# Where the last embedding product, the first gate product and the per-tile roots stand in the closing stage of a one-core decoder layer

## The chip, the cores and the metric

The kernel runs on one core of a Trainium2 chip. A core has TensorE (PE, matrix products), VectorE (DVE), ScalarE (ACT), GpSimd (POOL) and SyncE (SP, which issues most transfers); each runs its own instruction list in order, and they wait for one another through semaphores. The metric is the device time of the whole program in microseconds (us), as the median of several executions.

## The reference, cut to what matters

The program computes one decoder layer on x (512 tokens, 1024 channels): a mixing part (convolution and attention, then an output projection), a mixture of 32 experts with two per token, a gated embedding, and a last normalisation. The change lies in the last two:

```python
x = x + hier_moe(rms_norm(x, g_ffn[i]), ...)
gate = jax.nn.sigmoid(rms_norm(x, g_ple[i]) @ w_ple_gate[i] + b_ple_gate[i])
x = x + (p[i] @ w_ple_proj[i]) * gate
return rms_norm(x, g_final)
```

`p[i]` is 512 x 256, `w_ple_proj` 256 x 1024, `w_ple_gate` 1024 x 1024. `rms_norm` squares and sums a token's 1024 channels, takes the root of the mean plus a small number, and divides.

## The kernel before, in words

Tokens are cut into four tiles of 128 (t = 0 to 3), channels of an output into two halves of 512. Every engine's list is written out by hand; nothing is reordered by a scheduler, so the order in the code is the order on the engine. PSUM, where PE writes its products, is eight banks of 128 x 512; a table fixes which product uses which bank, and each bank has a semaphore for full and one for free.

The expert stage is a loop of passes. The last pass ends with the down products of PE (L1793). ACT and DVE copy their two banks to SBUF (L964, L1428), POOL scatters them to a buffer y_d in HBM, and SP reads y_d back as sorted rows (L701), four tiles of two parts. The closing stage is then:

- PE waits for both copies (`ya_ready`, `yd_ready`), and computes eight embedding products `ple(q)`, q = 0 to 7 (L1816, of two channel blocks each; q // 2 is the tile). ACT copies each out (L932).
- DVE adds the two expert parts to a tile of x (L1453, two instructions a tile). PE transposes the tile's rows (`turn_x2(t)`, L1848, eight transposes into two banks). ACT copies the transposed rows out rounded (x2_hi, L983), and DVE writes what the rounding left (x2_lo, L1460). ACT then squares and sums the tile and takes its root (`mean_root`, L800 and L802).
- PE computes eight gate products `product(q)` (L1837): q // 4 is the channel half and q % 4 the tile. Each is three groups of eight matmuls: high rows by high weights, low rows by high weights, high rows by low weights. The weights of a half are split into high and low by `split_gate` of ACT (L972) and of DVE (L1443). For the first half this lies before the embedding copies; for the second it comes on ACT behind the fourth tile's root, and on DVE behind its x2_lo. DVE handles no gate product before that second split is done.
- For each gate product, DVE multiplies by the tile's reciprocal root and adds the bias (L1488, which waits for the bank and frees it); ACT takes the sigmoid (L1003); DVE multiplies by the embedding (L1491) and adds to x (L1494); ACT squares and sums the 512 channels (`square_out`, L992).
- Once both halves of a tile are squared, ACT takes its last root (`final_root_of`, L999), and DVE its reciprocal (L1021) and two scalings of 512 columns (`final_out`, L1475); SP sends each of them out (L709).

Before, ACT takes the root of tile t one product late: behind the sigmoid of product 4 + t + 1, ahead of that product's square. DVE calls `final_out(t)` at the end of that same step, and so handles the next bank without waiting for a root in between. The sigmoid and the root lie in different activation tables, and an ACT_TABLE_LOAD stands where the function changes.

Of the kernel before, what the change touches and what calls it, by code (L numbers as in the profile page):

```python
# [55 lines left out]
FIXED = 3  # L56
SLOTS = 3
STRAIGHT = NE // 2 - 2
DOWN_PARTS = (2, 2, 4)
PAIRS = NE // 2  # L60
SORTED = PAIRS - FIXED
# [153 lines left out]
def build(nc, x, w_in, w_out, w_r, w_gate, w_up, w_down, w_pg, w_pp, pT, b_pg, g_final, prm, cst, out):  # L215
    ctx = ExitStack()
    with ctx:
        def sb(name, shape, dt=F32):
            return ctx.enter_context(nc.sbuf_tensor(name, shape, dt))
# [5 lines left out]
        def sem(name):  # L225
            return ctx.enter_context(nc.semaphore(name))
# [10 lines left out]
        xs = sb("xs", [P, TT, D])  # L237
# [27 lines left out]
        by8 = sb("by8", [P, 9, 2 * TT])  # L265
        gw = sb("gw", [P, 2, TT])
        sqh = sb("sqh", [P, 2, TT])
        key_col = sb("key_col", [P, 2])
        order = sb("order", [1, MOST, 2], I32)

# [56 lines left out]
        junk = ar(12288, D)  # L327
# [167 lines left out]
        xhi_ready = sem("xhi_ready")  # L495
        gated = sem("gated")
        squared = sem("squared")
        half_ready = sem("half_ready")
        final_root = sem("final_root")
        x3_ready = sem("x3_ready")  # L500
        o_ready = sem("o_ready")
# [290 lines left out]
        def _(act):  # L792
# [5 lines left out]
            def mean_root(which, t, unused):  # L798

                act.activation(unused, xs[:, t, :], ACT.Square, accum_out=sq[:, which, t:t + 1]).then_inc(root_ready, 1)  # L800
                act.wait_ge(root_ready, 2 * (which * TT + t) + 1)
                act.activation(ss[:, which, t:t + 1], sq[:, which, t:t + 1], ACT.Sqrt, scale=1.0 / D, bias=eps[:]).then_inc(root_ready, 1)  # L802
# [170 lines left out]
                                   scale=pr[:, Q_PLE + k:Q_PLE + k + 1]).then_inc(whi_ready, 1)  # L973

            split_gate(0)
            for q in range(2 * TT):
                ple_out(q)

            act.wait_ge(gathered[0], 16 * half + 16)
            for t in range(TT):  # L980
                for kh in range(2):
                    banks.wait_full(act, ("x2", t, kh))
                    act.activation(x2_hi[:, 4 * kh:4 * kh + 4, t * P:(t + 1) * P],  # L983
                                   bk(("x2", t, kh))[:].rearrange("p (k n) -> p k n", k=4), ACT.Copy).then_inc(xhi_ready, 1)
                mean_root(2, t, junk)
            split_gate(1)
            def square_out(q):

                half, t = q // TT, q % TT
                act.wait_ge(x3_ready, 2 * (q + 1))  # L990
                wait(act, squared, q)
                act.activation(junk[:, 0:512], xs[:, t, half * 512:(half + 1) * 512], ACT.Square, scale=1.0 / 32,  # L992
                               accum_out=sqh[:, half, t:t + 1]).then_inc(squared, 1)

            def final_root_of(t):

                act.wait_ge(half_ready, 1)
                act.wait_ge(squared, TT + t + 1)
                act.activation(ss[:, 3, t:t + 1], sqh[:, 1, t:t + 1], ACT.Sqrt, bias=sq[:, 3, t:t + 1]).then_inc(final_root, 1)  # L999

            for q in range(2 * TT):
                banks.wait_emptied(act, ("pgate", q))
                act.activation(sgate[:, q % 4, :], sgate[:, q % 4, :], ACT.Sigmoid).then_inc(gated, 1)  # L1003
                if q > TT:
                    final_root_of(q - TT - 1)
                square_out(q)
            final_root_of(TT - 1)


        @block.vector  # L1010
        def _(dve):
# [456 lines left out]
            def final_out(t):  # L1468

                if t == 0:  # L1470
                    dve.wait_ge(last_loaded, 16)
                dve.wait_ge(final_root, t + 1)
                recip(rs[:, 3, t:t + 1], ss[:, 3, t:t + 1])
                for cols in (slice(0, 512), slice(512, D)):
                    dve.scalar_tensor_tensor(out=xn_rows[:, t, cols], in0=xs[:, t, cols], scalar=rs[:, 3, t:t + 1],  # L1475
                                             in1=gfin[:, cols], op0=ALU.mult, op1=ALU.mult).then_inc(o_ready, 1)

            x3 = 0
            for q in range(2 * TT):
                half, t = q // TT, q % TT  # L1480
                name = ("pgate", q)
                cols = slice(half * 512, (half + 1) * 512)
                banks.wait_full(dve, name)
                if q == 0:
                    dve.wait_ge(bias_loaded, 16)
                if q >= 4:
                    dve.wait_ge(x3_ready, 2 * (q - 3))
                emptied(dve.scalar_tensor_tensor(out=sgate[:, q % 4, :], in0=bk(name)[:], scalar=rs[:, 2, t:t + 1],  # L1488
                                                 in1=brow[:, cols], op0=ALU.mult, op1=ALU.add), name)
                dve.wait_ge(gated, q + 1)  # L1490
                dve.tensor_tensor(sgate[:, q % 4, :], sgate[:, q % 4, :], plep[:, t, cols], ALU.mult).then_inc(x3_ready, 1)  # L1491
                x3 += 1
                dve.wait_ge(x3_ready, x3)
                dve.tensor_tensor(xs[:, t, cols], xs[:, t, cols], sgate[:, q % 4, :], ALU.add).then_inc(x3_ready, 1)  # L1494
                x3 += 1
                if q == TT:
                    dve.wait_ge(squared, TT)
                    dve.tensor_scalar(sq[:, 3, :], sqh[:, 0, :], EPS, None, ALU.add).then_inc(half_ready, 1)
                if q > TT:
                    final_out(t - 1)  # L1500
            final_out(TT - 1)


# [1 line left out]
        def _(pe):  # L1505
# [318 lines left out]
            def product(q):  # L1824

                half, t = q // TT, q % TT
                name = ("pgate", q)
                if t == 0:
                    pe.wait_ge(whi_ready, (half + 1) * DK)
                banks.wait_free(pe, name)  # L1830
                parts = ((wpg_hi[half], 0), (wpg_hi[half], 1), (wpg_lo[half], 0))
                for j, (w, rest) in enumerate(parts):
                    if t == 0 and j == 2:
                        pe.wait_ge(wlo_ready, (half + 1) * DK)
                    for k in range(DK):
                        lhs = x2_lo[t][:, k, :] if rest else x2_hi[:, k, t * P:(t + 1) * P]
                        ins = pe.matmul(bk(name)[:], lhs, w[:, k, :], start=(j == 0 and k == 0),  # L1837
                                        stop=(j == 2 and k == DK - 1))
                filled(ins, name)
# [49 lines left out]
```

## Time and profile before

| | us |
|---|---|
| median of 3 runs | 584.1 |
| lowest and highest | 583.13, 586.76 |
| the profiled execution | 583.52 |
| its span in the profile | 581.7 |
| PE busy | 505.3 (87%) |
| DVE busy | 294.8 (51%) |
| ACT busy | 184.9 (32%) |

The span runs from the first to the last recorded instruction; the execution's own time is 1.82 us longer. Busy shares are averages over stages with different limits. The closing stage, from the end of the last down product to the end of the span, takes the last 72 us. All times in the rows further down are counted from the start of the span.

### The profile page before, as it was taken

The numbers are of one execution on the slowest core, as the hardware profiler recorded it, in microseconds if no ns is written. First come the engines' busy times: TensorE is split into PE (matmuls) and PEld (weight loads), VectorE is DVE, ScalarE is ACT, GpSimd is POOL, SyncE is SP. The second block draws the span as 40 slices with busy tenths as digits, with TensorE's granted clock in tenths as the row PEclk, the third lists the DMA queues.
The fourth block names the chain that finished last, engine by engine and source line by source line (L and its number), as shares of the span: only waits on it lengthen the run. The fifth ranks groups of instructions, "written<-read, shape, count | busy, mean of one in ns | idle before, by whom it ended". The sixth has DMA issues, their size and how long they took to land.

```text
span 581.7 us, 8775 instructions
## 1 busy us (share of the span) xinstructions
PE 505.3 (87%) x3193; PEld 300.1 (52%) x3193; DVE 294.8 (51%) x558; ACT 184.9 (32%) x355; POOL 78.2 (13%) x91
## 2 busy tenths in 40 slices
PE   4999999997889979958999996887877888899994
PEld 4788888774556658854433332232222222237883
DVE  4329899999996963476221211111011111167676
ACT  6821411337775352332010100000000000066755
POOL 0740000000032040010211122011111001010000
PEclk9999999999889979988999999988888999899998
DMA  9931300445506065396999999999999899958003
GB/s 311 372 134 33 118 15 16 148 158 168 216 2 272 1 246 225 132 409 232 341 404 418 418 421 421 415 418 419 396 412 413 367 394 415 355 212 344 1 1 144
DMA packets 38071, 150.31 MB, mean 258 GB/s; under 512 B 5905, under 2 KB 10513, under 8 KB 26257
## 3 DMA queue, kind: packets, MB, share of 16 engines
q1 hardware_dynamic: 32416, 139.14, 61.3%
q0 software_dynamic: 5328, 10.50, 4.9%
q8 instruction: 25, 0.41, 0.3%
q10 hardware_dynamic: 288, 0.15, 0.1%
q14 instruction: 14, 0.11, 0.0%
HBM read 142.95 MB, written 14.68 MB: 271 GB/s over the span
## 4 chain that ended last, share of the span: by engine, by line
PE 53%; SPq 16%; DMA 12%; DVE 8%; ACT 5%; issue 4%; POOL 1%; DVEq 0%; POOLq 0%; ACTq 0%
PE bank L1528 15%; PE bank L1773 10%; DMA wring<-w_up_in 8%; PE bank L1837 8%; SPq L583 7%; PE bank L1630 5%; PE bank L1793 4%; PE bank L1554 4%; SPq L511 3%; SPq L603 2%; DMA wring<-w_in_in 2%; SPq L598 1%; PE bank L1671 1%; DMA wring<-y_d 1%; PE bank L1761 1%
## 5 line engine op out<-in xcount | busy, mean ns | idle before, releaser
L1773 PE MATMUL bank<-wring,arena 128*32 128x512 f32 x656 | 87.4, 658 | 19.9 <-DMA wring<-w_up_in 17.7
L1071 DVE SCALAR_TENSOR_TENSOR mix<-arena,pr,mix 128x512 f32<-128x512 f32 x120 | 85.6, 781 | 0.0
L1423 DVE TENSOR_TENSOR arena<-arena,bank 128x256 f32<-128x256 f32 x16 | 6.7, 421 | 138.7 <-ACT arena L958 138.7
L1773 PEld LDWEIGHTS bank<-wring,arena 128*32 128x32 f32 x656 | 25.8, 119 | 75.2 <-issue 68.7
L958 ACT ACTIVATE arena<-bank 128x256 f32<-128x256 f32 x16 | 6.2, 384 | 140.1 <-PE bank L1773 140.1
L1773 PE MATMUL bank<-mix,arena 128*32 128x512 f32 x240 | 38.6, 639 | 7.6 <-DMA arena<-w_up_in 7.6
L1793 PE MATMUL bank<-wring,arena 128*32 128x512 f32 x352 | 40.0, 595 | 5.3 <-ACT arena L961 5.3
L1773 PE MATMUL bank<-arena 128*32 128x512 f32 x80 | 38.6, 638 | 0.0
L1428 DVE COPY arena<-bank 128x512 f32<-128x512 f32 x16 | 11.1, 692 | 53.5 <-PE bank L1793 53.5
L1528 PE MATMUL bank<-hT_hi,win_hi 128*128 128x512 f32 x128 | 33.5, 398 | 1.2 <-DVE hT_lo L1049 0.6
L1528 PE MATMUL bank<-hT_lo,win_hi 128*128 128x512 f32 x128 | 31.7, 389 | 0.0
L1528 PE MATMUL bank<-hT_hi,win_lo 128*128 128x512 f32 x128 | 31.6, 389 | 0.0
L964 ACT ACTIVATE arena<-bank 128x512 f32<-128x512 f32 x16 | 9.6, 597 | 60.8 <-PE bank L1793 60.8
L1773 PEld LDWEIGHTS bank<-mix,arena 128*32 128x32 f32 x240 | 10.8, 116 | 34.6 <-issue 31.4
L1528 PEld LDWEIGHTS bank<-hT_hi,win_hi 128*128 128x128 f32 x128 | 23.6, 188 | 9.5 <-ACT hT_hi L820 1.9
L1528 PEld LDWEIGHTS bank<-hT_lo,win_hi 128*128 128x128 f32 x128 | 24.0, 188 | 5.0
L1528 PEld LDWEIGHTS bank<-hT_hi,win_lo 128*128 128x128 f32 x128 | 24.0, 188 | 5.0
L765 POOL COPY ycur<-tlist 128x1 int32 x16 | 2.9, 182 | 169.0 <-DVE arena L1428 169.0
L1793 PEld LDWEIGHTS bank<-wring,arena 128*32 128x32 f32 x352 | 10.3, 109 | 27.6 <-issue 20.5
L725 POOL TENSOR_TENSOR mixa_lo<-mix,mixa_hi 128x512 fp32r<-128x512 f32 x4 | 5.6, 1405 | 134.9 <-ACT mix L881 134.9
L1761 PEld LDWEIGHTS bank<-c,arena 128*128 128x128 f32 x136 | 15.3, 146 | 13.0 <-issue 12.6
L815 ACT ACTIVATE win_hi<-wring 128x1024 fp32r<-128x1024 f32 x20 | 20.0, 1072 | 5.5 <-DMA wring<-w_in_in 5.5
(260 smaller groups left out, 916.0 us busy)
## 6 DMA issues: line engine op xcount, KB each, us to landing
wring<-w_down_in SPq DMA_DIRECT2D x22, 1024.0 KB, 20.3
wring<-w_gate_in SPq DMA_DIRECT2D x21, 1024.0 KB, 15.5
wring<-w_up_in SPq DMA_DIRECT2D x21, 1024.0 KB, 19.1
wring<-w_in_in SPq DMA_DIRECT2D x3, 2048.0 KB, 14.5
arena<-w_down_in SPq DMA_DIRECT2D x5, 1024.0 KB, 13.8
mix<-w_up_in SPq DMA_DIRECT2D x5, 1024.0 KB, 13.1
arena<-w_up_in SPq DMA_DIRECT2D x5, 1024.0 KB, 20.1
mix<-w_gate_in SPq DMA_DIRECT2D x5, 1024.0 KB, 16.6
```

Of the source, the lines that this page charges most:

```text
L511: return eng.value_load(ap, min_val=least, max_val=most)
L583: sp.dma_start(up_w(w, a)[:, i], (w_gate, w_up)[i][bass.ds(expert(n, a), 1)].rearrange("e (p k) n -> p (e k) n", k=DK)).then_inc(up_loaded ...
L603: sp.dma_start(dn_w(w, a), src).then_inc(dn_loaded[w], 16)
L815: act.activation(win_hi[i][:, :, cols], win[i][:, :, cols], ACT.Copy).then_inc(win_hi_ready[i], 1)
L1071: ins = dve.scalar_tensor_tensor(out=mixc[:, mm, :], in0=u[:, mm, j:j + S], scalar=w, in1=mixc[:, mm, :], op0=ALU.mult, op1=ALU.add)
L1528: ins = pe.matmul(bk(name)[:], w[:, k, m * P:(m + 1) * P], h[:, k, :], start=(j == 0 and k == 0), stop=(j == 2 and k == DK - 1))
L1554: ins = pe.matmul(bk(("v", t))[:], h[:, k, t * P:(t + 1) * P], w[:, k, :], start=(j == 0 and k == 0), stop=(j == 2 and k == DK - 1))
L1630: ins = pe.matmul(bk(name)[:], src[:, m, t * P:(t + 1) * P], weight[:, m, half * 512:(half + 1) * 512], start=(j == 0), stop=(j == 3 * CM ...
L1761: ins = pe.transpose(pb[k // 4][:, k % 4 * P:(k % 4 + 1) * P], xg[:, s, k * P:(k + 1) * P], ident)
L1773: ins = pe.matmul(pb[2 + s][lo:hi, :], xgT[:, s, k, lo:hi], weights[:, :, k, :], start=(k == 0), stop=(k == DK - 1))
L1793: ins = pe.matmul(pb[6 + half][lo:hi, :], hidT[:, s, k, lo:hi], dn_cols(w, a, k, half), start=(k == 0), stop=(k == FK - 1))
L1837: ins = pe.matmul(bk(name)[:], lhs, w[:, k, :], start=(j == 0 and k == 0), stop=(j == 2 and k == DK - 1))
```

## The change

On PE, the waits for the two copies move from ahead of the first embedding product to ahead of the third (`ya_ready`) and the fourth (`yd_ready`). These are the products that write the banks concerned. The eighth embedding product moves behind the first tile's transposes. Each tile's transposes move behind the first group of the preceding tile's gate product, and the waits for x2_hi and x2_lo become separate.

```order
L1816 MATMUL bank<-wring 128x512 x16
L1848 MATMUL bank<-c,xs 128x128 x16
L1837 MATMUL bank<-wpg_hi_70,x_hi 128x512 x8
L1837 MATMUL bank<-wpg_hi_70,x_lo_75 128x512 x8
L1837 MATMUL bank<-wpg_lo_72,x_hi 128x512 x8
L1848 MATMUL bank<-c,xs 128x128 x8
L1837 MATMUL bank<-wpg_hi_70,x_hi 128x512 x8
```

Above is PE before, from the end of the expert loop; below is PE after the change, from the same place (L1857 are the embedding products, L1901 the transposes, L1889 the gate products).

```order
L1857 MATMUL bank<-wring 128x512 x4
L1864 REGISTER_ALU
L1857 MATMUL bank<-wring 128x512 x10
L1901 MATMUL bank<-c,xs 128x128 x8
L1857 MATMUL bank<-wring 128x512 x2
L1889 MATMUL bank<-wpg_hi_70,x_hi 128x512 x8
L1901 MATMUL bank<-c,xs 128x128 x8
L1889 MATMUL bank<-wpg_hi_70,x_lo_75 128x512 x8
L1889 MATMUL bank<-wpg_lo_72,x_hi 128x512 x8
```

The sixteen transposes in a row became eight and eight, with one embedding product and one group of a gate product in between; the number of matmuls is the same.

On ACT the root of a tile moves into the step of its own square, behind a small Sqrt that reads nothing new and calls for the table. The next two fences are ACT from the sigmoid of product 5 to the root of tile 1, before and after (L1003 and L1007 are the sigmoids, L992 and L996 the squares, L999 and L1003 of the second fence the roots, L1009 the small Sqrt).

```order
L1003 ACTIVATE wring<-wring 128x512
L999 ACT_TABLE_LOAD
L999 ACTIVATE ss<-sqh,sq 128x1
L992 ACTIVATE arena,sqh<-xs 128x512
L1003 ACT_TABLE_LOAD
L1003 ACTIVATE wring<-wring 128x512
L999 ACT_TABLE_LOAD
L999 ACTIVATE ss<-sqh,sq 128x1
```

After the change:

```order
L1007 ACTIVATE wring<-wring 128x512
L1009 ACT_TABLE_LOAD
L1009 ACTIVATE unused<-eps 128x1
L996 ACTIVATE arena,sqh<-xs 128x512
L1003 ACTIVATE ss<-sqh,sq 128x1
L1007 ACT_TABLE_LOAD
L1007 ACTIVATE wring<-wring 128x512
```

The root moved from ahead of a square to behind it.

On DVE the reciprocal and the two scalings of a tile move one product earlier: from behind the steps of the product that follows the tile's own second half, to ahead of them. Product 7 is handled in two parts of 256 columns. First DVE before, from the last addition of product 3 to the bias step of product 5, then the same stretch after the change (L1488 and L1510 are the bias steps, L1494 and L1516 the additions to x, L1498 and L1520 the constants from the first halves).

```order
L1494 TENSOR_TENSOR xs<-xs,wring 128x512
L1488 SCALAR_TENSOR_TENSOR wring<-bank,rs,wring 128x512
L1491 TENSOR_TENSOR wring<-wring,mix 128x512
L1494 TENSOR_TENSOR xs<-xs,wring 128x512
L1498 TENSOR_SCALAR sq<-sqh 128x4
L1488 SCALAR_TENSOR_TENSOR wring<-bank,rs,wring 128x512
```

After the change:

```order
L1516 TENSOR_TENSOR xs<-xs,wring 128x512
L1520 TENSOR_SCALAR sq<-sqh 128x4
L1510 SCALAR_TENSOR_TENSOR wring<-bank,rs,wring 128x512
L1513 TENSOR_TENSOR wring<-wring,mix 128x512
L1516 TENSOR_TENSOR xs<-xs,wring 128x512
L1041 RECIPROCAL rs<-ss 128x1
L1495 SCALAR_TENSOR_TENSOR arena<-xs,rs,wring 128x512 x2
L1510 SCALAR_TENSOR_TENSOR wring<-bank,rs,wring 128x512
```

The constants moved ahead of product 4, where they wait for the square of product 3; and the reciprocal and the scalings of tile 0, which waited for a root behind product 5, now stand ahead of the bias step of product 5.

The diff, cut to its core:

```diff
@@ ACT
-            for q in range(2 * TT):
+            for q in range(2 * TT - 1):
                 ple_out(q)
...
+                if t == 0:
+                    ple_out(2 * TT - 1)
                 mean_root(2, t, junk)
...
-                act.wait_ge(half_ready, 1)
-                act.wait_ge(squared, TT + t + 1)
+                act.wait_ge(half_ready, 1 if t < TT - 1 else 2)
+                act.wait_ge(squared, TT + t + 1 if t < TT - 1 else LAST + 2)
...
-            for q in range(2 * TT):
+            for q in range(LAST):
                 banks.wait_emptied(act, ("pgate", q))
                 act.activation(sgate[:, q % 4, :], sgate[:, q % 4, :], ACT.Sigmoid).then_inc(gated, 1)
-                if q > TT:
-                    final_root_of(q - TT - 1)
+                if q >= TT:
+                    act.activation(unused[:], eps[:], ACT.Sqrt)
                 square_out(q)
+                if q >= TT:
+                    final_root_of(q - TT)
+
+            for part in range(2):
+                cols = slice(part * 256, (part + 1) * 256)
+                if part == 0:
+                    act.wait_ge(part_ready, 1)
+                else:
+                    banks.wait_emptied(act, ("pgate", LAST))
+                act.activation(sgate[:, LAST % 4, cols], sgate[:, LAST % 4, cols], ACT.Sigmoid).then_inc(gated, 1)
+            act.activation(unused[:], eps[:], ACT.Sqrt)
+            for part in range(2):
+                act.wait_ge(x3_ready, 2 * (LAST + part + 1))
+                act.wait_ge(squared, LAST + part)
+                act.activation(junk[:, 0:256], xs[:, TT - 1, 512 + part * 256:768 + part * 256], ACT.Square, ...)
             final_root_of(TT - 1)
@@ DVE
-            for q in range(2 * TT):
+            for q in range(LAST):
                 half, t = q // TT, q % TT
                 name = ("pgate", q)
+                if q > TT:
+                    final_out(t - 1)
...
-                if q == TT:
+                if q == TT - 1:
                     dve.wait_ge(squared, TT)
                     dve.tensor_scalar(sq[:, 3, :], sqh[:, 0, :], EPS, None, ALU.add).then_inc(half_ready, 1)
-                if q > TT:
-                    final_out(t - 1)
+
+            final_out(TT - 2)
+            name, b = ("pgate", LAST), LAST % 4
+            banks.wait_full(dve, name)
...
+            for part in range(2):
+                cols = slice(part * 256, (part + 1) * 256)
+                ins = dve.scalar_tensor_tensor(out=sgate[:, b, cols], in0=bk(name)[:, cols], ...)
...
+            for part in range(2):
...
+                dve.wait_ge(gated, LAST + part + 1)
+                dve.tensor_tensor(sgate[:, b, cols], sgate[:, b, cols], plep[:, TT - 1, there], ALU.mult).then_inc(x3_ready, 1)
+                dve.wait_ge(x3_ready, x3 + 1)
+                dve.tensor_tensor(xs[:, TT - 1, there], xs[:, TT - 1, there], sgate[:, b, cols], ALU.add).then_inc(x3_ready, 1)
+                x3 += 2
+            dve.wait_ge(half_ready, 1)
+            dve.wait_ge(squared, LAST + 1)
+            dve.tensor_tensor(sq[:, 3, TT - 1:TT], sq[:, 3, TT - 1:TT], sq_part[:], ALU.add).then_inc(half_ready, 1)
             final_out(TT - 1)
@@ PE
-            pe.wait_ge(ya_ready, 2 * half)
-            pe.wait_ge(yd_ready, 2 * half)
-
             pe.wait_ge(xgT_ready, 4 * half + 2)
...
-            for q in range(2 * TT):
+            for q in range(2 * TT - 1):
+                if q == 2:
+                    pe.wait_ge(ya_ready, 2 * half)
+                if q == 3:
+                    pe.wait_ge(yd_ready, 2 * half)
                 ple(q)
...
             turn_x2(0)
-            for t in range(1, TT):
-                turn_x2(t)
-                for kh in range(2):
-                    banks.wait_emptied(pe, ("x2", t - 1, kh))
-                product(t - 1)
-            for kh in range(2):
-                banks.wait_emptied(pe, ("x2", TT - 1, kh))
-            for q in range(TT - 1, 2 * TT):
-                product(q)
+            ple(2 * TT - 1)
+            for t in range(TT):
+                product(t, 0, 1)
+                if t < TT - 1:
+                    turn_x2(t + 1)
+                product(t, 1, 3)
+            for q in range(TT, 2 * TT):
+                product(q, 0, 3)
```

`product(q, lo, hi)` issues groups lo to hi - 1 of the three; its first group waits for x2_hi only, its second for x2_lo.

## Rows read from the trace of the kernel before

**Rows 1.** Page, part 1: busy us (share of the span) and instructions.
```profile
PE 505.3 (87%) x3193; PEld 300.1 (52%) x3193; DVE 294.8 (51%) x558; ACT 184.9 (32%) x355; POOL 78.2 (13%) x91
```

**Rows 2.** Chain of waits, 500 to 582 us: start, us, what.
```profile
540.32 32.67 PE bank L1837 x144
...
573.01 0.76 DVE wring L1488
...
577.79 0.75 DVE arena L1475
```

**Rows 3.** Timeline, PE: start, us, engine, line, operation, xcount [idle before <-releaser].
```profile
510.79 13.97 PE L1816 MATMUL bank<-wring 128*128 128x512 f32 x32 [1.11 <-DVE arena L1428]
...
527.38 2.09 PE L1837 MATMUL bank<-wpg_hi,x_hi 128*128 128x512 f32 x8 [0.55 <-issue]
...
533.75 2.07 PE L1837 MATMUL bank<-wpg_hi,x_hi 128*128 128x512 f32 x8
...
539.28 1.03 PE L1848 MATMUL bank<-c,xs 128*128 128x128 f32 x8
...
571.00 1.98 PE L1837 MATMUL bank<-wpg_lo,x_hi 128*128 128x512 f32 x8
```

**Rows 4.** Windows: stretch, its length, busy of PE, PEld, DVE, ACT, POOL, clock, DMA.
```profile
540.00:550.00 10.00, 10.00 (x47) 8.31 (x46) 8.06 (x16) 9.16 (x15) 0.00 (x0) 1.00 0.01 2
```

**Rows 5.** Timeline, DVE and ACT ahead of the gate steps.
```profile
519.56 2.60 DVE L1453 SCALAR_TENSOR_TENSOR xs<-wring,gw,xs 128x1024 f32<-128x1024 f32 x2 [3.19 <-DMA wring<-y_d]
...
542.28 5.00 ACT L972 ACTIVATE wpg_hi<-arena,pr 128x512 fp32r<-128x512 f32 x8
...
548.40 0.75 DVE L1488 SCALAR_TENSOR_TENSOR wring<-bank,rs,wring 128x512 f32<-128x512 f32 x1
...
551.18 0.74 DVE L1488 SCALAR_TENSOR_TENSOR wring<-bank,rs,wring 128x512 f32<-128x512 f32 x1
```

**Rows 6.** Timeline, DVE and ACT, product 6 to the last tile's root.
```profile
567.57 0.75 DVE L1488 SCALAR_TENSOR_TENSOR wring<-bank,rs,wring 128x512 f32<-128x512 f32 x1 [0.48 <-PE bank L1837]
568.36 0.63 ACT L1003 ACTIVATE wring<-wring 128x512 f32<-128x512 f32 x1 [1.06 <-DVE wring L1488]
...
569.01 1.28 ACT L999 ACT_TABLE_LOAD   x1
569.02 0.69 DVE L1491 TENSOR_TENSOR wring<-wring,mix 128x512 f32<-128x512 f32 x1 [0.70 <-ACT wring L1003]
...
569.75 0.69 DVE L1494 TENSOR_TENSOR xs<-xs,wring 128x512 f32<-128x512 f32 x1
570.30 0.29 ACT L999 ACTIVATE ss<-sqh,sq 128x1 f32<-128x1 f32 x1
570.50 0.62 ACT L992 ACTIVATE arena<-xs 128x512 f32<-128x512 f32 x1
570.63 0.16 DVE L1021 RECIPROCAL rs<-ss 128x1 f32<-128x1 f32 x1 [0.19 <-ACT ss L999]
...
570.83 1.42 DVE L1475 SCALAR_TENSOR_TENSOR arena<-xs,rs,wring 128x512 f32<-128x512 f32 x2
...
571.23 1.28 ACT L1003 ACT_TABLE_LOAD   x1
...
575.94 0.61 ACT L992 ACTIVATE arena<-xs 128x512 f32<-128x512 f32 x1
...
576.27 1.42 DVE L1475 SCALAR_TENSOR_TENSOR arena<-xs,rs,wring 128x512 f32<-128x512 f32 x2
...
576.74 0.30 ACT L999 ACTIVATE ss<-sqh,sq 128x1 f32<-128x1 f32 x1
577.60 0.15 DVE L1021 RECIPROCAL rs<-ss 128x1 f32<-128x1 f32 x1
```

**Rows 7.** Timeline, DVE and ACT instructions of 256 columns that read PSUM.
```profile
504.57 0.42 DVE L1423 TENSOR_TENSOR arena<-arena,bank 128x256 f32<-128x256 f32 x1 [11.08 <-ACT arena L958]
...
505.52 0.38 ACT L961 ACTIVATE arena<-bank 128x256 f32<-128x256 f32 x1 [0.98 <-PE bank L1784]
```

More of the change, by code:

```diff
@@ L58 @@
 STRAIGHT = NE // 2 - 2
+LAST = 2 * TT - 1
 DOWN_PARTS = (2, 2, 4)
@@ L267, in build @@
         sqh = sb("sqh", [P, 2, TT])
+        sq_part = sb("sq_part", [P, 1])
         key_col = sb("key_col", [P, 2])
@@ L497, in build @@
         squared = sem("squared")
-        half_ready = sem("half_ready")
+        half_ready, part_ready = sem("half_ready"), sem("part_ready")
         final_root = sem("final_root")
@@ L995, in final_root_of @@
             def final_root_of(t):
-                act.wait_ge(half_ready, 1)
-                act.wait_ge(squared, TT + t + 1)
+                act.wait_ge(half_ready, 1 if t < TT - 1 else 2)
+                act.wait_ge(squared, TT + t + 1 if t < TT - 1 else LAST + 2)
                 act.activation(ss[:, 3, t:t + 1], sqh[:, 1, t:t + 1], ACT.Sqrt, bias=sq[:, 3, t:t + 1]).then_inc(final_root, 1)
-            for q in range(2 * TT):
+            for q in range(LAST):
                 banks.wait_emptied(act, ("pgate", q))
                 act.activation(sgate[:, q % 4, :], sgate[:, q % 4, :], ACT.Sigmoid).then_inc(gated, 1)
-                if q > TT:
-                    final_root_of(q - TT - 1)
+                if q >= TT:
+                    act.activation(unused[:], eps[:], ACT.Sqrt)
                 square_out(q)
+                if q >= TT:
[11 more added lines that the diff above has]
+                act.wait_ge(squared, LAST + part)
+                act.activation(junk[:, 0:256], xs[:, TT - 1, 512 + part * 256:768 + part * 256], ACT.Square, scale=1.0 / 32,
+                               accum_out=(sq_part[:] if part == 0 else sqh[:, 1, TT - 1:TT])).then_inc(squared, 1)
             final_root_of(TT - 1)
@@ L1495, in _ @@
                 x3 += 1
-                if q == TT:
+                if q == TT - 1:
                     dve.wait_ge(squared, TT)
                     dve.tensor_scalar(sq[:, 3, :], sqh[:, 0, :], EPS, None, ALU.add).then_inc(half_ready, 1)
-                if q > TT:
-                    final_out(t - 1)
+            final_out(TT - 2)
+            name, b = ("pgate", LAST), LAST % 4
+            banks.wait_full(dve, name)
+            dve.wait_ge(x3_ready, 2 * (LAST - 3))
+            for part in range(2):
+                cols = slice(part * 256, (part + 1) * 256)
+                ins = dve.scalar_tensor_tensor(out=sgate[:, b, cols], in0=bk(name)[:, cols], scalar=rs[:, 2, TT - 1:TT],
+                                               in1=brow[:, 512 + part * 256:768 + part * 256], op0=ALU.mult, op1=ALU.add)
+                if part == 0:
+                    ins.then_inc(part_ready, 1)
+                else:
+                    emptied(ins, name)
+            for part in range(2):
+                cols = slice(part * 256, (part + 1) * 256)
+                there = slice(512 + part * 256, 768 + part * 256)
+                dve.wait_ge(gated, LAST + part + 1)
[6 more added lines that the diff above has]
+            dve.tensor_tensor(sq[:, 3, TT - 1:TT], sq[:, 3, TT - 1:TT], sq_part[:], ALU.add).then_inc(half_ready, 1)
             final_out(TT - 1)
@@ L1820, in _, with product @@
             pe.wait_ge(ple_loaded, 32)
-            for q in range(2 * TT):
+            for q in range(2 * TT - 1):
[3 more added lines that the diff above has]
+                    pe.wait_ge(yd_ready, 2 * half)
                 ple(q)
-            def product(q):
+            def product(q, lo, hi):
                 half, t = q // TT, q % TT
                 name = ("pgate", q)
-                if t == 0:
-                    pe.wait_ge(whi_ready, (half + 1) * DK)
-                banks.wait_free(pe, name)
+                if lo == 0:
+                    if t == 0:
+                        pe.wait_ge(whi_ready, (half + 1) * DK)
+                    banks.wait_free(pe, name)
                 parts = ((wpg_hi[half], 0), (wpg_hi[half], 1), (wpg_lo[half], 0))
-                for j, (w, rest) in enumerate(parts):
+                for j in range(lo, hi):
+                    w, rest = parts[j]
                     if t == 0 and j == 2:
                         pe.wait_ge(wlo_ready, (half + 1) * DK)
+                    if half == 0 and j == 1:
+                        for kh in range(2):
+                            banks.wait_emptied(pe, ("x2", t, kh))
                     for k in range(DK):
+                        if half == 0 and j == 0 and k % 4 == 0:
+                            pe.wait_ge(xhi_ready, 2 * t + k // 4 + 1)
                         lhs = x2_lo[t][:, k, :] if rest else x2_hi[:, k, t * P:(t + 1) * P]
@@ L1838, in product @@
                                         stop=(j == 2 and k == DK - 1))
-                filled(ins, name)
+                if hi == 3:
+                    filled(ins, name)
             def turn_x2(t):
```

## Prediction

> **What bounds the kernel now.** The page's busy shares give PE 87% and DVE and ACT far less [rows 1], but that is an average over the whole program, and the change touches only the last 72 us. The chain of waits over that stretch says which engine holds the end: PE from 540.32 for 32.67 us, without a break [rows 2], then DVE at 573.01, and at 577.79 the last two scalings, 3.91 us before the span ends at 581.7. The reader should see that one change of hands, PE to DVE at 573.01, decides the time: whatever makes DVE start the bias step of product 7 (call this moment B7) earlier or later moves the end by as much. The timeline then shows how near the other two engines are. DVE starts its first bias step at 548.40 [rows 5], some 15 us after PE completed that product [rows 3], because the second split of weights stands ahead of it. It works through this backlog at 2.78 us a product (548.40 to 551.18). PE delivers one each 5.5 us, so DVE has caught up by product 6: there DVE is idle for 0.48 us before its bias step, waiting for PE [rows 6]. So DVE and ACT have little slack at the end, and the length of one of their steps is what to cost.
>
> **The PE part.** Each piece from the timeline.
>
> - Start. PE idles 1.11 us ahead of the embedding products [rows 3]. With the waits two products later this idle goes to between 0 and 1.11. Seven products at 13.97 / 8 = 1.75 us end between 521.9 and 523.0. The first tile's sum on DVE is ready at 519.56 + 2.60 = 522.16 [rows 5]; so the transposes start at 522.2 at best, and up to 0.8 later. I take 522.3, since the banks of the first two products need neither copy.
> - A gate product alone takes 533.75 to 539.28, 5.53 us; with a tile's transposes 527.38 to 533.75, 6.37 [rows 3]; so the transposes cost 0.84, and a third of a product 1.84.
> - New time of the fourth tile's transposes: 522.3 + 0.84 + 1.75 (eighth embedding product, which hides the wait for x2_hi; the idle of 0.55 at 527.38 goes) = 524.9 for the first gate product; + 2 x 6.37 + 1.84 = 539.5. Before it was 539.28, so 0.2 later: the group that was moved ahead of the transposes takes nearly all that was won.
> - PE's end: from 539.28 to 571.00 + 1.98 = 572.98 it took 33.7. A third of a product less lies behind those transposes now: 539.5 + 33.7 - 1.8 = 571.4, a gain of 1.6 us for PE itself.
>
> ACT's second split starts 3.00 us behind those transposes (542.28) and DVE's first bias step 6.12 behind that. With nothing else in that stretch changed, the first bias step is at 548.6. Its ends are 548.4 (idle gone, transposes unhindered) and 549.2 (nothing won at the start). The clock granted to PE is 1.00, the upper of its two levels, 2.4 GHz [rows 4], and I keep it: PE idles less than before.
>
> **The DVE and ACT part.** Here a new ring of waits arises. From product 5 on, DVE may start a bias step only behind the scalings of the tile before, these wait for the tile's root, and the root now waits for the square of the product just handled. One round, start to start, from the rows of product 6 and the last tile [rows 6]:
>
> - bias step to sigmoid, 567.57 to 568.36: 0.79
> - sigmoid to square, 568.36 to 570.50: 2.14. Two paths take the same time: 0.65 for the sigmoid, 1.28 for the table, 0.20 for the small root; or the multiply and the addition on DVE (ends at 569.75 + 0.69 = 570.44)
> - square to a root that needs it, 575.94 to 576.74: 0.80
> - root to reciprocal, 570.30 to 570.63: 0.33; reciprocal to scaling 0.20
> - two scalings to the next DVE instruction, 576.27 to 577.60: 1.33
>
> The sum is 5.59 us. Before, the first four could run beside PE, and the bias step waited for PE alone. The switch back to the sigmoid's table starts 0.3 behind the root, at 3.24 of the round counted from the sigmoid, and ends at 4.52; the next sigmoid is at 5.59. So it costs nothing, by a cover of 1.07 us. The small root was not there before: at least 0, at most its 0.29; I take 0.20, the distance from root to square. It matters little, since the DVE path is as long.
>
> Product 3 gets a wait too: DVE waits for its square before it can make the constants. Behind DVE's wait stands the bias step of product 4. Bias step 3 to 4 is 0.79 + 2.14 + 0.80 + 0.05 = 3.78 in place of 2.78.
>
> The times of the bias steps: product 3 at 548.6 + 3 x 2.78 = 556.9; product 4 at 560.7; product 5 at 566.3; product 6 at 571.9; product 7 (B7) at 577.5. PE delivers product 7 at 571.4, 6 us too early to matter. Against 573.01, B7 is 4.5 us late. PE's gain of 1.6 reaches the end nowhere.
>
> **The tail.** From B7 to the last scalings it was 577.79 - 573.01 = 4.78. In two parts: half a bias step of 0.42 [rows 7] and a hop of 0.04, the second half's sigmoid at 0.86, its end at 1.24 with 0.38 for 256 columns [rows 7], the table to 2.54, the small root to 2.74. A square that is followed by one that waits for it costs 0.80 less the 0.25 of the missing columns, 0.55: twice, 3.84. Then 0.33 and 0.20: 4.37, a gain of 0.4. The addition of the part sum is hidden beside the second square. The output behind it (3.91) stays.
>
> The sum is +4.5 - 0.4 = +4.1: span 585.8, and with the 1.82 around it 587.6. The profiled execution before (583.52) is 0.58 below the median shown, so a median comes out at 588.2. I say 588.0.
>
> A rule that would change the sum: in the Trainium skill's "ScalarE: Activation LUTs", section "What ACT_TABLE_LOAD costs", every switch to another set costs the load and a drain, together about 2.66 us. By it one round would be 7.3 us and the median about 594. Here the sigmoid of product 6 ends at 568.99 and the root that stands behind the load starts at 570.30, 1.31 later, so the trace gives 1.28 and a rest of 0.03 [rows 6], and the sum goes by that.
>
> **Rivals.**
>
> - PE stays the bound, as a reader of the chain alone would expect. Then B7 is at 571.4, and the end 1.6 + 0.4 = 2.0 earlier: 582.1. It speaks for it that DVE is free for about half of the stretch. It would need rounds of (571.4 - 560.7) / 3 = 3.6 us or less, against 5.59 of instructions and hops that depend on one another. Some overlap that I read wrongly could give part of it. Chance 0.08.
> - A switch of tables costs more in the new place than in the old. The work across it is now the sigmoid and a root with nothing in flight, before a root with its inputs long there. If a switch held ACT for two loads, 2.56 us, the square would come at 3.41 of a round, the root at 4.21, the sigmoid's table would be there at 7.07, and rounds would be 1.48 longer: 3 x 1.48 + 1.28 in the tail = +5.7, 593.7. It decides for "slower" from about 0.45 us a switch on. The rows show 0.03. The rule on the drain, above, is this rival's stronger form. Chance 0.05.
>
> The forecast has 0.87. A measurement of this kernel tells about 1% (5.8 us) from no change; the forecast is +0.7%, on the slow side and within it. Hops between engines that are longer than I read them, and executions well above the profiled one, as the 586.76 shown before, could bring the case of the forecast over that (0.08); with the second rival that makes 0.13 for slower by over 1%. The first rival is itself within 1%, so faster by over 1% gets 0.02, and within 1% 0.85. The range: the forecast with its start between -0.2 and +0.6, hops of 0.1 to 0.3 in each of four rounds, and a spread of 1 us of the median gives 585.8 to 590.2. The first rival, the second and the ends of the first make up what lies outside.
>
> **What would show it.** Right: the bias steps of products 5, 6 and 7 stand 5.6 us apart, with DVE idle before its reciprocals for about 1.2 us, released by ACT's root; PE's last matmul ends near 571.4, and the chain of waits runs through DVE and ACT from about 542, not through PE. The first bias step is near 548.6. Last scalings at 4.4 behind B7. Wrong: bias step 7 released by PE; a round that differs from 5.6 by more than 0.3; a load of the sigmoid's table that ends after the bias step before it; a first bias step later than 549.2, which would mean that the moved transposes wait for something not costed here.

## The result, and the profile after

| | before | changed |
|---|---|---|
| median, us | 584.15 (8 runs, 580.71 to 586.76) | 588.17 (8 runs, 585.60 to 591.90) |
| ratio, 95% interval | | 1.008 (1.005 to 1.0109) |
| profiled execution, its span | 583.52, 581.7 | 588.73, 586.9 |

The change makes the kernel slower by 0.8%, and a ratio of 1 (no change) lies outside the interval. The chain of waits of the changed kernel, 500 to 587 us (start, us, what), has another shape than before [rows 2]:

```profile
540.76 0.45 PE bank L1901 x4
541.23 1.09 ACT x_hi L985 x2
...
549.79 0.67 DVE wring L1510
...
568.85 1.28 ACT L1009
570.14 0.20 ACT unused L1009
570.34 0.70 ACT arena L996 x2
571.13 0.30 ACT ss L1003
571.46 0.17 DVE rs L1041
...
572.32 0.75 DVE arena L1495
573.07 0.67 DVE wring L1510
```

PE leaves the chain at 541, with the transposes of the fourth tile, and doesn't come back. Before, it held the chain until 573. The rows from 568.85 are one round: table, small root, square, root, reciprocal, scaling, next bias step. The timeline of DVE and ACT in the changed kernel, from product 5 to 7, answers to [rows 6]:

```profile
567.42 0.75 DVE L1510 SCALAR_TENSOR_TENSOR wring<-bank,rs,wring 128x512 f32<-128x512 f32 x1
568.20 0.63 ACT L1007 ACTIVATE wring<-wring 128x512 f32<-128x512 f32 x1 [1.11 <-DVE wring L1510]
...
571.46 0.16 DVE L1041 RECIPROCAL rs<-ss 128x1 f32<-128x1 f32 x1 [1.18 <-ACT ss L1003]
571.66 1.42 DVE L1495 SCALAR_TENSOR_TENSOR arena<-xs,rs,wring 128x512 f32<-128x512 f32 x2
572.99 0.75 DVE L1510 SCALAR_TENSOR_TENSOR wring<-bank,rs,wring 128x512 f32<-128x512 f32 x1
...
577.02 0.16 DVE L1041 RECIPROCAL rs<-ss 128x1 f32<-128x1 f32 x1 [1.17 <-ACT ss L1003]
...
578.55 0.87 DVE L1528 SCALAR_TENSOR_TENSOR wring<-bank,rs,wring 128x256 f32<-128x256 f32 x2
```

The bias steps are 5.57 and 5.56 us apart. DVE stands idle before each reciprocal for 1.2 us, released by ACT's root; before, it was PE that released the bias step. PE's last rows in the changed kernel:

```profile
570.65 1.98 PE L1889 MATMUL bank<-wpg_lo,x_hi 128*128 128x512 f32 x8
```

They end at 572.63, 5.9 us ahead of the bias step that takes their result.

**A common zero for the traces.** The executions differ by some us before the closing stage is reached, so stages have to be compared from a common event. The end of the last down product is a bad one. In the changed kernel DVE's copy of it starts at 509.38, and the first tile's sum 11.37 us later; before it was 9.82. A better one is the issue of the load of x by SP, at 482.68 before and at 483.77 after: from there to the first tile's sum it is 36.88 and 36.98 us (why is shown with the experiments). From that event:

| from the issue of x's load, us | before | predicted | changed |
|---|---|---|---|
| first transposes | 41.9 | 39.6 | 39.6 |
| PE's end | 90.3 | 88.7 | 88.9 |
| first bias step | 65.7 | 65.9 | 65.9 |
| bias step of product 7 | 90.3 | 94.8 | 94.8 |
| last scalings | 95.1 | 99.2 | 99.2 |
| end of the span | 99.0 | 103.1 | 103.1 |

The predicted column is the prediction's own moments less 482.68. A second trace of each kernel gave 98.96 and 102.88 for the last line.

### The profile page after: what moved, and what is told of

It reads as the page before. It is cut to its first block, busy times and chain, and to the rows that moved or that the text cites. A ratio compares the mean times of both kernels' runs of the same rounds, so it can differ in the third digit from the quotient of the medians.

```text
span 586.9 us, 8794 instructions
## 1 busy us (share of the span) xinstructions
PE 503.8 (86%) x3193; PEld 297.0 (51%) x3193; DVE 295.2 (50%) x562; ACT 188.6 (32%) x364; POOL 78.3 (13%) x91
## 4 chain that ended last, share of the span: by engine, by line
PE 48%; SPq 16%; DMA 12%; DVE 10%; ACT 8%; issue 5%; POOL 1%; DVEq 0%; POOLq 0%; ACTq 0%
PE bank L1572 15%; PE bank L1817 10%; DMA wring<-w_up_in 8%; SPq L585 7%; PE bank L1674 5%; PE bank L1837 4%; PE bank L1598 4%; SPq L513 3%; SPq L605 3%; PE bank L1889 2%; DMA wring<-w_in_in 2%; SPq L600 1%; PE bank L1715 1%; PE bank L1805 1%; PE bank L1642 1%
## 5 line engine op out<-in xcount | busy, mean ns | idle before, releaser
L1817 PE MATMUL bank<-mix,arena 128*32 128x512 f32 x240 | 40.2, 660 | 7.8 <-DMA arena<-w_up_in 7.8
L1817 PE MATMUL bank<-arena 128*32 128x512 f32 x80 | 40.1, 660 | 0.0
```

The source lines that it names most:

```text
L1817: ins = pe.matmul(pb[2 + s][lo:hi, :], xgT[:, s, k, lo:hi], weights[:, :, k, :], start=(k == 0), stop=(k == DK - 1))
```

## The experiments

The theory: a ring of dependent steps through DVE and ACT, which the change closes, holds the end. The rival: the new order on PE and the later feed that comes with it. A ratio is that to the kernel before on the same chip, with its 95% interval.

**PE's order alone.** ACT's and DVE's loops over the gate products are those of the kernel before. The cut is against the changed kernel.

```diff
-            for q in range(LAST):
+            for q in range(2 * TT):
                 banks.wait_emptied(act, ("pgate", q))
                 act.activation(sgate[:, q % 4, :], sgate[:, q % 4, :], ACT.Sigmoid).then_inc(gated, 1)
-                if q >= TT:
-                    act.activation(unused[:], eps[:], ACT.Sqrt)
+                if q > TT:
+                    final_root_of(q - TT - 1)
                 square_out(q)
```

> The change's order on TensorE alone; the roots, the scalings and the last product's steps are those of the kernel before. Theory (a ring of dependent steps through ScalarE and VectorE, 5.6 us a round, holds the end after the change): there is no ring here, TensorE keeps the end. The bias step of product 7 is released by TensorE, the tail behind it is 4.8 us as before, and the time is 0.4 to 1.6 us below the kernel before (1.6 if the first tile's sum is ready as early as before, 0.4 if the scattered rows come 1.2 us late as in the changed kernel's trace). Rival (the order on TensorE and the later feed of rows and weights make the change slower): the first bias step stays about 41 us behind the last down product's copy, and the time is 2 us or more above the kernel before.

Ratio 0.9977 (0.9955 to 0.9999), 582.53 against 583.72 us. The end is 97.66 us behind the issue of x's load, 1.36 less than before. The first bias step is 40.21 us behind the copy of the last down product, as the rival expects, but the time is lower and not higher. So this distance costs nothing.

> TensorE's new order alone, timed again with more rounds. Its trace is 1.4 us shorter than that of the kernel before, from the issue of x's load to the end. If that is all there is: a ratio of 0.9976, with an interval that leaves 1 out. If the first timing was luck: 1.000.

A second timing gave 0.9993 (0.9972 to 1.0014), its trace 97.61. The traces repeat to 0.05 us and say -1.4; the timings say between -0.1% and -0.2%, and the second one does not tell it from no change. By the traces it is the fastest kernel here that computes the whole result; the timings can't tell it from the kernel with PE's waits alone, further down (0.9983). One part of the expectation fell: PE doesn't release the last bias step. Timeline of DVE in that kernel:

```profile
566.27 0.74 DVE L1492 SCALAR_TENSOR_TENSOR wring<-bank,rs,wring 128x512 f32<-128x512 f32 x1
...
569.51 1.42 DVE L1479 SCALAR_TENSOR_TENSOR arena<-xs,rs,wring 128x512 f32<-128x512 f32 x2
570.85 0.74 DVE L1492 SCALAR_TENSOR_TENSOR wring<-bank,rs,wring 128x512 f32<-128x512 f32 x1
```

No idle time stands before the bias steps. They are 4.58 us apart, less than PE's 5.4 for a product, because DVE is still catching up; it reaches the last one 0.26 us behind PE's end. DVE and ACT are as late as PE here: by this trace nothing more could be won on PE.

**Roots, scalings and the two-part product alone** ("roots alone" below), with PE's order of the kernel before.

```diff
-            ple(2 * TT - 1)
-            for t in range(TT):
-                product(t, 0, 1)
-                if t < TT - 1:
-                    turn_x2(t + 1)
-                product(t, 1, 3)
-            for q in range(TT, 2 * TT):
-                product(q, 0, 3)
+            for t in range(1, TT):
+                turn_x2(t)
+                for kh in range(2):
+                    banks.wait_emptied(pe, ("x2", t - 1, kh))
+                product(t - 1)
+            for kh in range(2):
+                banks.wait_emptied(pe, ("x2", TT - 1, kh))
+            for q in range(TT - 1, 2 * TT):
+                product(q)
```

> The change's roots, scalings and two-part last product; the order on TensorE is that of the kernel before. Theory of the ring: bias steps of products 5, 6 and 7 are 5.6 us apart, that of product 4 is 3.8 us behind that of product 3, TensorE ends some 5 us ahead of the last bias step, and the time is 3.5 to 4.5 us above the kernel before. Rival (order on TensorE): within 1 us of the kernel before.

Ratio 1.0081 (1.0052 to 1.0109), the whole of the change's loss. The bias steps of 4 to 7 stand 3.73, 5.64, 5.57 and 5.56 us behind their predecessors, and PE ends 4.3 us ahead of the last one. Timeline of DVE in that kernel:

```profile
568.78 0.75 DVE L1508 SCALAR_TENSOR_TENSOR wring<-bank,rs,wring 128x512 f32<-128x512 f32 x1
...
572.82 0.16 DVE L1039 RECIPROCAL rs<-ss 128x1 f32<-128x1 f32 x1 [1.18 <-ACT ss L1001]
573.02 1.42 DVE L1493 SCALAR_TENSOR_TENSOR arena<-xs,rs,wring 128x512 f32<-128x512 f32 x2
574.35 0.74 DVE L1508 SCALAR_TENSOR_TENSOR wring<-bank,rs,wring 128x512 f32<-128x512 f32 x1
```

The end of the span is 103.22 us behind the issue of x's load, 4.2 more than before. The rival falls.

**Scalings late**: one link of the ring undone.

```diff
-                if q > TT:
-                    final_out(t - 1)
                 cols = slice(half * 512, (half + 1) * 512)
...
                     dve.tensor_scalar(sq[:, 3, :], sqh[:, 0, :], EPS, None, ALU.add).then_inc(half_ready, 1)
+                if q > TT:
+                    final_out(t - 1)
 
-            final_out(TT - 2)
...
+            final_out(TT - 2)
             dve.wait_ge(half_ready, 1)
```

> The changed kernel with one thing undone: VectorE scales a tile only behind the steps of the next product (for the third tile, behind the additions of product 7), so no bias step waits for a root; ScalarE's order stays. Theory of the ring in its full form: VectorE leaves the ring, but ScalarE alone still needs per round sigmoid 0.65, load 1.28, small root 0.2, square 0.8, root 0.3, load 1.28 = 4.5 us from product 4 on, and it starts late, so the sigmoids of 5, 6 and 7 are 4.5 us apart and product 7's is some 2 to 3 us behind TensorE; time 2.5 to 3.5 us below the changed kernel, 1 to 2 us above the kernel before. Simple form of the theory (only VectorE's wait for the root counts): TensorE is the bound again, 5 to 6 us below the changed kernel. Rival (order on TensorE): no difference from the changed kernel.

Ratio 1.0025 (1.0003 to 1.0047): 0.55% below the changed kernel's 1.008, still above the kernel before. The full form is right. In the trace the last bias step is 2.50 us behind PE's end, and from the first bias step to the end of the span it is 34.6 us, against 37.2 in the changed kernel. Timeline of ACT (the table for the sigmoid, and the sigmoid, of products 5 and 6):

```profile
564.38 1.28 ACT L1007 ACT_TABLE_LOAD   x1
565.67 0.63 ACT L1007 ACTIVATE wring<-wring 128x512 f32<-128x512 f32 x1
...
568.92 1.28 ACT L1007 ACT_TABLE_LOAD   x1
570.21 0.63 ACT L1007 ACTIVATE wring<-wring 128x512 f32<-128x512 f32 x1
```

No idle stands before the sigmoids, and they are 4.54 us apart. ACT alone is the ring now, with two table loads in it. In the changed kernel the load of the sigmoid's table was free; take DVE's wait for the root out of the ring, and it is the next thing on the path.

**Constants late.**

```diff
-                if q == TT - 1:
+                if q == TT:
                     dve.wait_ge(squared, TT)
```

> The changed kernel with the constants from the first halves made behind product 4 again, where their squares are long done. Theory: the bias step of product 4 is 2.8 us behind that of product 3, not 3.7, the ring behind it keeps its rounds of 5.6, and the last bias step is 1.0 us nearer to the first one (27.8 us, not 28.8). Rival (the ring swallows it, because something else holds its start): no difference.

One execution, so there is no ratio. Its trace: 2.78 to bias step 4, then 5.63, 5.57, 5.57; 27.89 from the first bias step to the last, against 28.84. The wait cost 0.95 us; the prediction gave it 1.00 (3.78 in place of 2.78).

**No small root.**

```diff
-                if q >= TT:
-                    act.activation(unused[:], eps[:], ACT.Sqrt)
                 square_out(q)
...
-            act.activation(unused[:], eps[:], ACT.Sqrt)
             for part in range(2):
```

> The changed kernel without the four small roots, so that the load of the root's table comes behind the square and not beside VectorE's multiply and addition. Theory of the ring: each round takes 1.2 us more (6.8), three of them and 0.6 in the tail, 4.2 us above the changed kernel. Rival (TensorE or the feed holds the end): no difference, since ScalarE is idle over half of the stretch.

Ratio 1.015 (1.0097 to 1.0204), from four executions. Timeline of ACT in one round:

```profile
573.22 0.63 ACT L996 ACTIVATE arena<-xs 128x512 f32<-128x512 f32 x1 [1.48 <-DVE xs L1513]
573.76 0.19 ACT L996 ACTIVATION_READ_ACCUMULATOR arena<-xs 128x1 f32 x1
574.02 1.28 ACT L1003 ACT_TABLE_LOAD   x1
575.31 0.29 ACT L1003 ACTIVATE ss<-sqh,sq 128x1 f32<-128x1 f32 x1
...
577.95 0.63 ACT L1007 ACTIVATE wring<-wring 128x512 f32<-128x512 f32 x1 [1.04 <-DVE wring L1507]
```

ACT now idles 1.48 us for DVE's addition and loads the table behind the square. Rounds are 6.93, 6.84 and 6.84 us, and the tail is 0.63 longer; from the first bias step to the last scalings that makes 4.5 us more than in the changed kernel. A cost put into the ring comes back three times over and once more in part; so it is the ring that holds the end. It also shows that the small root is the good part of the change's ACT order.

**Product 7 whole**, handled in the loop as products 4 to 6 are.

```diff
-LAST = 2 * TT - 1
+LAST = 2 * TT
...
-            for part in range(2):
-                cols = slice(part * 256, (part + 1) * 256)
-                if part == 0:
-                    act.wait_ge(part_ready, 1)
...
-            final_out(TT - 2)
-            name, b = ("pgate", LAST), LAST % 4
```

> The changed kernel with product 7 handled whole, in the same way as products 4 to 6. Prediction's term: two parts gain 0.4 us against the tail before, so this would be 0.4 slower. Rival: the gain of the tail comes only from the third tile's scalings standing ahead of it; a whole product costs 0.79 + 2.14 + 0.80 + 0.33 + 0.20 = 4.26 us from the bias step to the last scalings, against 4.45 in the changed kernel's trace, so this is 0.2 us faster. By the trace, from the last bias step to the last scalings; the medians can't tell.

Ratio 1.0056 (1.0033 to 1.0079). From the last bias step to the last scalings 4.24 us, against 4.45 in two parts. The rival is right: the two parts cost 0.2 us. The median says more (0.2%), but its interval overlaps that of the changed kernel.

**PE's waits alone**, in the kernel before.

```diff
-            pe.wait_ge(ya_ready, 2 * half)
-            pe.wait_ge(yd_ready, 2 * half)
-
             pe.wait_ge(xgT_ready, 4 * half + 2)
...
             for q in range(2 * TT):
+                if q == 2:
+                    pe.wait_ge(ya_ready, 2 * half)
+                if q == 3:
+                    pe.wait_ge(yd_ready, 2 * half)
                 ple(q)
```

> The kernel before with one edit: TensorE's waits for the two copies stand ahead of the third and fourth embedding product. Theory: the embedding products start 0.1 us behind the last down product and not 1.1 to 1.5, but the transposes start when the first tile's sum is ready, so TensorE's end moves by at most the 1.4 us that it is late there now; 0 to 1 us below the kernel before. Rival (the early start makes the scatter of the last rows slower, 5.4 us against 3.9 in the kernel before): 1 us or more above it, with the first sum 11.3 us behind the copy, not 9.8.

Ratio 0.9983 (0.9960 to 1.0006). The scatter took 5.38 us and the first sum came 11.24 behind the copy, the rival's signs, yet nothing got slower: the end is 98.79 behind the issue of x's load, 0.2 less than before. How these signs and the time go together is shown by the next two experiments.

**Second traces.**

> The changed kernel once more, for a second trace of it. If its late feed is a property of the change: the scatter of the last rows again takes about 5.4 us and the first tile's sum starts 11.3 us behind the copy. If it is scatter between executions: nearer to the 3.9 and 9.8 of the kernel before, and the first bias step at 39 us behind the copy.

> The kernel before once more, for a second trace. If the distance from the issue of x's load to the first tile's sum is set by the queues of transfers, it is 36.9 us again, whatever the last pass of the experts takes (8.5 us in the first trace, 7.1 in the changed kernel's), and the time from that issue to the end of the span is 99.0 us again.

The changed kernel again has 5.39 us of scatter and 11.26 to the first sum; the kernel before again has 9.85. In the kernel before, the scatter is shorter (3.92 us), but the copy comes later, for another reason. Timeline of PE, last pass of the experts, second trace of the kernel before, and its granted clock in the window (the column 0.83, ahead of the transfers' 0.95):

```profile
495.28 8.47 PE L1773 MATMUL bank<-wring,arena 128*32 128x512 f32 x64 [2.92 <-DMA wring<-w_up_in]
```

```profile
495.30:503.70 8.40, 8.40 (x65) 2.12 (x65) 0.00 (x0) 0.00 (x0) 0.42 (x1) 0.83 0.95 344
```

In the changed kernel (first trace) the same pass:

```profile
496.65 7.07 PE L1817 MATMUL bank<-wring,arena 128*32 128x512 f32 x64 [1.24 <-DMA wring<-w_up_in]
```

```profile
496.70:503.70 7.00, 7.00 (x65) 1.98 (x65) 0.00 (x0) 0.00 (x0) 1.20 (x2) 1.00 0.96 345
```

PE idled 2.9 us for weights and then ran part of the pass at the lower of its two clock levels, 1.2 GHz; after an idle of 1.2 it ran all of it at 2.4. The pass is 1.4 us shorter in the second case, the copy that much earlier, and the first sum comes no sooner: 36.5 to 37.4 us behind the issue of x's load in eleven of the twelve traces with that load whole, whichever the pass was. In the twelfth (scalings late, the pass took 9.96 us) it came at 38.05, 9.22 behind the copy, because there the copy was what was late. So the first sum seems to have two bounds: the loads that were queued before the scatter, and some 9 us from the copy (9.22 here, 8.93 in the next experiment).

**Less to load**, on PE's order alone.

```diff
-            sp.dma_start(xs[:], x1_rows).then_inc(x1_loaded, 16)
+            sp.dma_start(xs[:, 0:1], x1_rows[:, 0:1]).then_inc(x1_loaded, 16)
```

> TensorE's new order alone, as before, with three of the four tiles of x (1.5 MB) not loaded again ahead of the closing stage; the last tiles' x is left out of the result. Theory (the scattered rows wait behind loads that are still in the queues, so the first tile's sum comes 36.9 us behind the issue of x's load however early the last down product ends): with less in the queues the scatter takes 3.9 us or less instead of 5.4, the first sum starts 9 to 10 us behind the copy instead of 11.2, the transposes at 12 instead of 13.9, and the span from the issue of that load is 1.5 to 2 us shorter than 97.7. Rival (TensorE's early start makes the scatter slow): scatter 5.4, first sum 11.2, no change of the span from the issue.

Timeline of PE at the start of the closing stage, first with x loaded whole (PE's order alone), then with a quarter of it:

```profile
514.87 5.42 PE L1817 MATMUL bank<-wring 128*128 128x512 f32 x12 [0.43 <-ACT mix L934]
521.35 1.09 PE L1861 MATMUL bank<-c,xs 128*128 128x128 f32 x8 [1.06 <-DVE xs L1457]
```

```profile
508.66 12.28 PE L1817 MATMUL bank<-wring 128*128 128x512 f32 x28
520.78 1.04 PE L1861 MATMUL bank<-c,xs 128*128 128x128 f32 x8
```

The two idles go, the scatter takes 3.2 us, the first sum starts 8.93 us behind the copy, the transposes at 11.99, as the theory has it. The span from the issue fell by 0.85 us to 96.81, not by 1.5 to 2: the last pass took 8.77 us in this trace, so the copy itself came 1.1 later. Ratio 0.9965 (0.9944 to 0.9986); the kernel with x loaded whole had 0.9993 in the same series.

A late copy alone gives the same signs: in scalings late, with x loaded whole, the two idles are gone too and the scatter takes 3.1 us. So the fair comparison is with a trace whose copy came at nearly the same time. In the kernel before, copy and first sum are 27.06 and 36.88 us behind the issue of x's load; here they are 26.70 and 35.63. The sum gained 0.9 us over what the copy did, and in no trace with the load whole did it come before 36.5. That is what shows the load as a bound.

## Why the prediction was right

588.0 was forecast, 588.17 measured. That the medians agree to 0.2 us is partly luck: the interval of the ratio runs from 2.9 to 6.4 us of loss. What bears the forecast out is the mechanism in the traces, whose end moved by 4.11 us against 4.1. By its steps:

- **PE's part**: the fourth tile's transposes were to come 0.2 us later and the first bias step with them. Measured 65.94 against 65.72 from the common event, 0.2. PE itself was to end 1.6 earlier; it did by 1.4 (88.86 against 90.30).
- **One sentence in it was too simple.** I let the embedding products run without a stop once their waits had moved. They start at once, but stop for 0.4 us at the fifth for its bank (ACT copies out late, since its split waited 1.27 us for weights) and 1.2 us for the first sum. The transposes still came on the predicted moment, because the first tile's sum, and not PE, sets them; that bound was in the prediction. It took the moment of that sum over from the kernel before without a reason, though, and this was luck: the copy came 1.45 us earlier and the scatter took 1.5 us longer.
- **The ring**: 5.59 forecast, 5.56 to 5.65 measured, in four kernels. Its cover is right too: the sigmoid's table is there 1.1 us early (ACT idles 1.11 and 1.04 before the sigmoids).
- **The wait for the constants**: 3.78 forecast, 3.73 measured; undone, 0.95 us come back. From the first bias step to the last it is 28.84, with 28.9 forecast.
- **The tail**: 4.37 forecast, 4.45 measured, a gain of 0.33 us over 4.78. But the reason was half wrong. The gain comes from the third tile's scalings, which now stand ahead of the last bias step: before, the last root was there at 577.04 and DVE took its reciprocal at 577.60, behind those scalings. Whole, the tail is 4.24. The cut into two parts loses 0.2 us: the first square starts 2.74 us behind the bias step, not 2.90, but the two squares in a row take 1.19 until the root (581.29 to 582.48), where a whole one takes 0.81.
- **The range** doesn't follow from its three terms. The hops it names only add, so the terms give 586.8 (start 0.2 earlier, spread 1 us) to 590.8, not 585.8 to 590.2. The measured median lies in both.
- **The rivals**: PE stayed the bound in no trace with the ring. A table switch takes the 1.28 us of its load and 0.03 us beside it: sigmoid's end to small root 1.31 (568.83 to 570.14). The Trainium skill's "ScalarE: Activation LUTs", section "What ACT_TABLE_LOAD costs", has about 2.66 us a switch; no switch here shows it.

The first rival has a lesson beyond its number. In the kernel before, DVE and ACT seemed to have slack of 0.5 and 0.8 us a product at the end. PE's order alone shows what lies behind that: PE's end came 1.55 us earlier, the last bias step 1.32, and no idle time stood before DVE's bias steps any more. By that trace a larger gain on PE would have been lost even without the ring.

## What to carry to other kernels

Before a dependent step is moved nearer to its source ("as soon as its input is there"), write down the loop of waits that it closes and add it up, start to start: if one round is longer than the bound engine's period, the engine that was idle half of the time becomes the bound. A result that is needed only at the end may trail by one round at little cost: before, the trailing roots cost 0.5 us in the tail (4.78 against 4.24), and taking them at once cost 3.3 between the first bias step and the last (27.89 against 24.61, without the wait for the constants). Compare stages of two traces from an event that both the moved and the unmoved work depend on; measured from the last down product, this change seemed to cost 5.6 us instead of 4.1.

## What the hardware showed that was not expected

- The scatter of 128 rows issued by POOL took the longer, the sooner it followed the load of x. Issued 27.4 to 27.9 us behind the issue of that load (eight traces) it took 5.3 to 6.1 us, at 29.1 to 29.4 (two of the kernel before, one of roots alone) 3.7 to 4.0, at 30.9 (scalings late) 3.1. In eleven of these twelve traces it ended 0.1 to 0.7 us behind the landing of x's load (514.44 and 514.94 in the trace of PE's order alone), in scalings late 1.2 us. With 1.5 MB less in the queues it took 3.2 (510.89 to 514.07, where SP issues the loads of the sorted rows).
- The last pass of the experts took 8.5 to 8.8 us in all three traces with PE's waits at the old place (two of the kernel before, one of roots alone) and 7.07 in eight of ten with the waits moved, though those waits stand behind that pass. The pass before it has the counterpart: in all thirteen traces exactly one of the two ran in part at 1.2 GHz (mean granted clock 0.71 to 0.83) and took 8.4 to 10.0 us, and the other ran at 2.4 GHz and took 7.07 or 7.08. The last pass starts 12.3 to 13.2 us behind the issue of x's load, either way; where PE is idle before it, it waits for the weights. So a slow pass before it leaves a short idle (1.6 us at most), and a fast one leaves 2.9 to 3.7. Which of the two passes gets the lower clock was not settled; the idle ahead of a pass alone doesn't say it, as the pass before the last ran at 1.00 behind an idle of 2.22 us in the kernel before, and at 0.81 behind 2.23 in the changed kernel.
